# Feed-forward and MLP up projections by seven quarter products instead of eight

## What is computed

```python
h = rms_norm(x, norm_mlp[layer])
x = x + jnp.square(jax.nn.relu(h @ w_up[layer])) @ w_down[layer]      # MLP, 4096 wide
...
def swiglu(h, w_gate, w_up, w_down):
    return (jax.nn.silu(h @ w_gate) * (h @ w_up)) @ w_down
...
c_act = jax.nn.silu(c)
for l in range(DEPTH_2):
    mod = (c_act @ w_ada[l] + b_ada[l]).reshape(B, N_MOD, D_MODEL)    # N_MOD = 9
    h = modulate(rms_norm_2(x, norm_gain[l, 0]), mod[:, 0], mod[:, 1])
    x = x + 0.5 * mod[:, 2][:, None, :] * swiglu(h, ffn_w_gate[l, 0], ffn_w_up[l, 0], ffn_w_down[l, 0])
    ...                                                               # mixer, then the second swiglu
```

## Time and profile before

| | |
|---|---|
| median of 3 runs | 3504.78 us |
| profiled execution, first to last instruction | 3498.8 us |
| PE busy | 3407.7 us (97%), 17034 matmuls |
| POOL busy | 2369.8 us (68%) |
| DVE busy | 1179.6 us (34%) |
| ACT busy | 885.8 us (25%) |
| DMA | 388.09 MB, mean 111 GB/s |

### The profile page before, as it was taken

The page is one execution under the profiler, slowest core; times in us unless marked ns, Lnnn a source line. Parts: engine busy times, 40 slices in busy tenths (PEclk is TensorE's granted clock), DMA queues, the critical chain, the costliest instruction groups (busy, mean ns, idle before and its releaser), DMA issues.

```text
span 3498.8 us, 42521 instructions
## 1 busy us (share of the span) xinstructions
PE 3407.7 (97%) x17034; PEld 2738.7 (78%) x17034; DVE 1179.6 (34%) x2514; ACT 885.8 (25%) x1876; POOL 2369.8 (68%) x1242
## 2 busy tenths in 40 slices
PE   8888999999999999999999999999999999999999
PEld 6655777988898888667779888888887677798887
DVE  6554332433443234442223111332244422241111
ACT  2656551211120102354312000210012543221000
POOL 7515447787778776645677877687775546678775
PEclk9999999999999999999999999999999999999999
DMA  3222213444535442212232222254432122223222
GB/s 142 68 69 82 67 62 108 149 171 170 185 127 204 168 166 94 73 58 85 85 106 96 97 97 96 83 220 165 171 126 73 67 76 79 82 97 106 98 98 73
DMA packets 104773, 388.09 MB, mean 111 GB/s; under 512 B 12017, under 2 KB 12401, under 8 KB 98433
## 3 DMA queue, kind: packets, MB, share of 16 engines
q1 hardware_dynamic: 88272, 292.76, 24.4%
q10 hardware_dynamic: 16304, 92.62, 7.0%
HBM read 383.20 MB, written 2.13 MB: 110 GB/s over the span
## 4 chain that ended last, share of the span: by engine, by line
PE 92%; DVE 4%; ACT 3%; issue 1%; ACTq 0%; DVEq 0%
PE psum L1234 28%; PE psum L1236 27%; PE psum L1235 27%; PE psum L1307 2%; PE psum L1349 2%; PE psum L1324 2%; PE psum L1293 1%; DVE rs_t L1695 1%; ACT s_sb L1477 0%; DVE s_sb L1736 0%; ACT L1477 0%; ACT s_sb L1495 0%; PE psum L1407 0%; PE psum L1285 0%; DVE n_sum L1906 0%
## 5 line engine op out<-in xcount | busy, mean ns | idle before, releaser
L1202 POOL TENSOR_TENSOR w_hi<-raw,ones 128x1024 fp32r<-128x1024 f32 (+2 forms) x593 | 1041.3, 1756 | 990.4 <-PE psum L1236 981.2
L1205 POOL TENSOR_TENSOR w_lo<-raw,w_hi 128x1024 fp32r<-128x1024 f32 (+2 forms) x593 | 1315.1, 2218 | 46.5
L1234 PE MATMUL psum<-h_hi,w_hi 128*128 128x512 f32 (+2 forms) x2912 | 1143.4, 393 | 19.4 <-DVE r L1711 9.4
L1236 PE MATMUL psum<-h_hi,w_lo 128*128 128x512 f32 (+2 forms) x2912 | 1105.3, 380 | 0.0
L1235 PE MATMUL psum<-h_lo,w_hi 128*128 128x512 f32 (+2 forms) x2912 | 1104.8, 379 | 0.0
L1234 PEld LDWEIGHTS psum<-h_hi,w_hi 128*128 128x128 f32 (+1 forms) x2912 | 550.2, 189 | 156.6 <-issue 35.9
L1236 PEld LDWEIGHTS psum<-h_hi,w_lo 128*128 128x128 f32 (+1 forms) x2912 | 549.7, 189 | 106.6
L1235 PEld LDWEIGHTS psum<-h_lo,w_hi 128*128 128x128 f32 (+1 forms) x2912 | 550.9, 189 | 103.3 <-issue 9.0
L1234 PE MATMUL psum<-a_hi,w_hi 128*128 128x512 f32 (+1 forms) x1064 | 392.5, 369 | 0.0
L1235 PE MATMUL psum<-a_lo,w_hi 128*128 128x512 f32 (+1 forms) x1064 | 391.8, 368 | 0.0
L1236 PE MATMUL psum<-a_hi,w_lo 128*128 128x512 f32 (+1 forms) x1064 | 391.8, 368 | 0.0
(11 more groups left out here) (198 smaller groups left out, 3299.5 us busy)
## 6 DMA issues: line engine op xcount, KB each, us to landing
raw<-weights_dram SPq DMA_DIRECT2D x487, 512.0 KB, 3.3
ada_t<-ada_dram ACTq DMA_DIRECT2D x48, 1536.0 KB, 7.1
raw<-weights_dram SPq DMA_DIRECT2D x76, 256.0 KB, 2.6
raw<-weights_dram SPq DMA_DIRECT2D x32, 384.0 KB, 2.9
bias_t<-biases_dram ACTq DMA_DIRECT2D x36, 256.0 KB, 2.9
bias_t<-cum_dram ACTq DMA_DIRECT2D x16, 256.0 KB, 3.9
out_dram<-x SPq DMA_DIRECT2D x8, 256.0 KB, 2.1
raw<-weights_dram SPq DMA_DIRECT2D x4, 408.0 KB, 3.1
```

Of the source, the lines that this page charges most:

```text
L1202: nc.gpsimd.tensor_tensor(high, piece, ones[:, 0:1].to_broadcast([P, n]), ALU.mult)\
L1205: nc.gpsimd.tensor_tensor(w_lo[:, p % NR, 0:n], piece, high.bitcast(F32), ALU.subtract)\
L1234: mm(dst, lh, rh, start=first, stop=False)
L1236: return mm(dst, ll, rh, start=False, stop=last)
```

## The change

Gate and up groups after the first four are made in *sets* of four: two pairs (in a feed-forward part two gates and two ups, in the MLP two and two ups). A pair is a product of a 2 by 2 array of weight quarters (two output chunks by two halves of the 1024 input features) with a 2 by 2 array of quarters of `h` (halves of the features by halves of the tokens), made by seven products instead of eight. A product takes four chunks with three matmuls of 256 columns each (L1538 to L1540), 12 in all, so a set takes 14 products and 168 matmuls of 256 columns where it was 96 of 512. There are 7 sets in the MLP and 10 in each of the four feed-forward parts, 47 in all.

- Sums of quarters of `h` (`t_new`, `t_hi`, `t_lo`) are made once for each norm, in four steps (`tsum`, `tlow`): four DVE instructions of 256 columns, an ACT copy of 1024 and a DVE subtraction of 1024 in each. The scaled input stands in SBUF (`n_out`) instead of PSUM, since it is needed again.
- Sums of weight quarters are made in PSUM banks 0 and 1: ACT moves a quarter there, DVE adds (S3, S1, S2, S4), ACT or POOL makes the high and DVE or POOL the low part of each of the 14 operands. An operand takes one of the six slots (512 columns high, 512 low).
- Partial results are kept by ACT (`keep`) and added by DVE (`c22`, `c1`) ahead of the gate and the product.
- `norm_rest` interleaves four first groups instead of three (banks 6, 7, 4, 5).
- The condition's sums, now two for each load of 1 MB, stand only between down groups (ten in each of three parts of the MLP; 9, 9 and 0, then 9, 9 and 0, then 6, 0 and 0 in the feed-forward parts), and its silu is made in banks 0 and 1 anew for each of these parts. The first two loads are issued behind the last set of the first part.

```diff
@@ norm_rest: the sums of h behind the second half of the norm
+    sums = quarter_sums(m) if m.quartered else iter(())
     for c in range(KC):
         for g in firsts:
             mm(g, c, c + 1, 1)
-        next(second, None)
+        if next(second, None) is None:
+            next(sums, None)
+    for _ in sums:
+        pass
@@
+def with_ada(groups, n, stop):
+    def condition():
+        tick("c_made")
+        put("cond", [take(b) for b in SUM_BANKS], TOTAL["cond_loaded"])
+    out = [condition]
+    for i, g in enumerate(groups):
+        out += [lambda: ada_sum(stop)] * sum(6 * k // n == i for k in range(n)) + [g]
+    return out
@@
+BY = dict(P1=("pool", "pool"), P2=("pool", "pool"), P5=("act", "dve"), P6=("act", "dve"), P7=("act", "pool"),
+          P3=("act", "dve"), P4=("pool", "pool"))
...
+    for what in PRODUCTS:
+        for p in pairs:
+            p.ops[what].done = tick("product_done")
+            put("product", p.ops[what])
...
+            elif what == "P3":
+                p.c1 = tick("combined")
+                put("c1", p)
+                result(p, 0)
+            elif what == "P4":
+                result(p, 1)
@@ ffn
+        for t in range(first, chunks, 2):
+            kinds = [[(kind, l, n, at + t + i) for i in TWO] for kind in ("fg", "fu")]
+            banks = SET_BANKS[(chunks - t) // 2 % 2 == 0]
+            jobs.append(lambda kinds=kinds, t=t, banks=banks: new_set(kinds, ((t, t + 1),) * 2, banks, m))
...
+        if part == 0 and stop:
+            jobs += [ada_load, ada_load]
+        if not closes:
+            groups = down_groups(keys, chunks, "a", (l, 2 * n))
+            jobs += with_ada(groups, ada[part], stop) if ada[part] else groups
@@ where the scaled input stands (norm_tile, which L1671, L1425 and L1678 of before use)
-            return bank(m.nt[c % 2])[:, columns(half)]
+            return n_out[:, c, columns(half)] if m.quartered else bank(m.nt[c % 2])[:, columns(half)]
@@ which steps come when an operand's slot is free (place - 6 used)
+    for step in ORDER:
+        if step[0] in ("prep", "mm", "product"):
+            yield from ready()
+        yield step
@@ PE
+            def product(op):
+                pair, what, m = op.pair, op.what, op.pair.norm
+                E.wait_at(op.low)
...
+                for k in range(KC // 2):
+                    if what in ("P1", "P2", "P3"):
+                        c, cs = k + KC // 2 * (what != "P1"), columns(int(what == "P3"))
+                        hi, lo = h_hi[:, c, cs], h_lo[:, c, cs]
+                    else:
+                        E.wait_ge("t_lo", m.sums + k + 1)
+                        j = dict(P5=0, P6=1, P7=2, P4=3)[what]
+                        hi, lo = t_hi[:, k, j, :], t_lo[:, k, j, :]
...
+                    mm(dst, wh[:, w], hi, start=start, stop=False, skip_group_check=True)
+                    mm(dst, wh[:, w], lo, start=False, stop=False, skip_group_check=True)
+                    ins = mm(dst, wl[:, w], hi, start=False, stop=stop, skip_group_check=True)
@@ ACT
+            def operand(op):
+                gate, up = SETS[op.pair.made // 8]
+                if (op.what, op.pair) == ("P2", up):
+                    move(gate)
+                elif (op.what, op.pair) == ("P5", gate):
+                    move(up)
@@ DVE
+            def quarter_sum(m, k):
...
+                if k >= 2:
+                    E.wait_ge("t_lo", m.sums + k - 1)
+                v.tensor_tensor(t[0], n_out[:, k, far], n_out[:, k, near], ALU.subtract)
...
+            def first_sums(pair):
+                a, _, c, d = quarters(pair)
+                E.wait_at(loaded(pair.pieces[0]))
+                E.wait_ge("moved", pair.moved)
+                v.tensor_tensor(c, sums(pair), a, ALU.add).then_inc(sem["sums_made"], 1)
+                E.wait_at(summed(pair, "S3"))
+                v.tensor_tensor(sums(pair), sums(pair), d, ALU.add).then_inc(sem["sums_made"], 1)
+            def operand(op):
+                gate, up = SETS[op.pair.made // 8]
+                if (op.what, op.pair) == ("P2", up):
+                    first_sums(gate)
+                elif (op.what, op.pair) == ("P5", gate):
+                    first_sums(up)
+                if op.low[0] == "low_dve":
+                    E.wait_at(op.high)
+                    v.tensor_tensor(low_of(op), sums(op.pair), high_of(op).bitcast(F32), ALU.subtract)
+                if op.what in ("P5", "P6"):
+                    next_sum(op.pair, "S2" if op.what == "P5" else "S4")
```

More of the change, by code:

```diff
@@ L308, with quartered @@
     used: int = 0
+    products: int = 0
+    sums: int = 0
+    @property
+    def quartered(self):
+        return self.which == ("mlp",) or len(self.which) == 2 and self.which[1] != 1
     def square_bank(self, c, half):
@@ L376, in norm_chunks, with quarter_sums @@
         yield c
+def quarter_sums(m):
+    m.sums = TOTAL.get("t_lo", 0)
+    for k in range(KC // 2):
+        assert tick("t_sum") == tick("t_hi") == m.sums + k + 1
+        put("tsum", m, k)
+        yield k
+        if k:
+            put("tlow", m, k - 1, tick("t_lo"))
+    put("tlow", m, KC // 2 - 1, tick("t_lo"))
 def in_banks(groups, banks):
@@ new lines @@
+@dataclass(eq=False)
+class Operand:
+    what: str
+    pair: object
+    place: int
+    high: tuple = None
+    low: tuple = None
+    done: int = 0
+@dataclass(eq=False)
+class Pair:
+    side: int
+    banks: tuple
+    norm: Norm
+    made: int
+    pieces: tuple = ()
+    before: tuple = ()
+    ops: dict = None
+    former: object = None
+    sums_before: tuple = None
+    moved: int = 0
+    p1: int = 0
+    p5: int = 0
+    u2: int = 0
+    c22: int = 0
+    c1: int = 0
+@dataclass(eq=False)
```

420 lines of the change are left out of this document (326 added, 94 removed).

## The result

The changed kernel takes 3593.22 us (median of 4 runs, 3590.35 to 3604.75), the kernel before on the same chip 3502.61 us (4 runs). The ratio is 1.0263, with a 95% interval of 1.0245 to 1.0281: 2.6% slower. The forecast was 3557 us, range 3482 to 3610: sign and range held, and 36 of the 91 us were missing. The time lies nearer to the 3608 us of the rival in which every later set waits than to the forecast; only the trace tells the two apart.

The account below looks back on a forecast made before the run. PE, busy 97% of the span, was taken to bound the kernel. 3498.8 - 75.2 + 1.6 + 16 + 65.6 + 10 + 34 = 3550.8 us for the span, 6.0 more for the median: 3557 us, range 3482 to 3610.

Parts of the forecast that it names:

- the rival in which every later set waits: Feed-forward sets: if each hand-over costs 0.15 us more, sets lose 2.1 us, 51 us more, 3608 us; chance 0.14.
- The matmuls: PE in the 47 sets: 1.60 us gained each, 75.2 us; halves in the fourth first group cost 1.6 us.
- Inside the sets: Operand waits within sets: POOL 8 us over 12 parts, MLP's second P5 6, late `a_lo` 2; sum 16 us.
- The norms: Two PE waits at each of five norms, for bank 5 and for quarter sums (`t_lo`) in P5: 65.6 us.
- The condition's sums: Down groups: additions that empty banks stand behind load sums, so PE waits 34 us; 8 with quick loads.
- the loads are quick: Rival on the condition's loads: at 3.3 us each they cost 8 us, 3531 us; lower part of the forecast's 0.60.
- The clock: Idle PE then runs at half clock, one stretch a norm and a few in down groups: 10 us, bounds 0 and 30.
- The signs that I named: PE idle 4 to 5 us before first groups are well begun, released by addition or `n_sum`; 7 to 12 in P5, by `t_lo`.
- sign of a wrong forecast: PE idle under 3 us a norm at `t_lo`, or waits for POOL's or DVE's operands above 30 us in all.
- DVE in time at the norms: Rival at the norms: DVE makes quarter sums early enough, norm and clock terms go, 3481 us, faster; chance 0.20.

Follow-up runs that it names:

- x11: Kernel before the change, feed-forward sets changed except plain first sets; early loads, first-half `h_lo` from PSUM, coefficient instructions spread: 3466.3 us, 0.9906 of before.
- x5: Changed kernel with the first set after each of five norms made of four plain groups of 512 columns: 3566.8 us, 1.0191 of the kernel before.
- x4: Changed kernel with the eight small coefficient instructions issued one by one, a down group apart: 3583.8 us, 1.0239 of the kernel before.
- x9: Changed kernel with product P2 of both pairs made three times in the first set after each norm: 3589.7 us, 1.0261 of the kernel before.
- x8: Changed kernel with the MLP as before; in feed-forwards a plain first set after the norm and two early loads: 3489.7 us, 0.9965 of before.

## Why the prediction was right, and what it sized wrong

- *The matmuls*, 75.2 us: 0.120 us a step in the sets, as forecast. x11, where the waits are few, is 34 us faster than before.
- *Inside the sets*, 16 us: 7.1 for POOL as worked out (12 x 0.6, which I had rounded up to 8), and the MLP's second P5 9.9 us (two waits of 1.7 and 1.6 in three parts; I had one of 2.1). With the late `a_lo` some 21. The rival with waits in every later set is refuted: feed-forward sets wait for nothing but POOL.
- *The norms*, 65.6 us: 14 in first halves where I had 23, 28.5 at `t_lo` and P5 where I had 43: 42 us of recorded waits. Both mechanisms are there. The lock meets only some of the `h_lo`: I had each of the first five wait, and in the MLP's norm two of eight take 2.3 and 2.2 us, two 0.9 and four 0.48. At `t_lo` the price was nearly right: 5.25 us of rows in ff(0,0), but 6.3 us of delay where I had 7.4. That the order of place 1 makes these waits, with an idle DVE in it, is read from the timelines; x5 takes the wait away by giving PE other work, and no run moved the quarter sums ahead of the products.
- *The condition's sums*, 34 us: 43 us of waits in the down groups. By MLP parts it was 8.2, 8.1 and 14.8 us where I had 11.2, 6.5 and 6.5; the feed-forwards had 12 where I had 10. Three things were off. The first two loads of a phase I gave 9.3 us, but 2 MB at the 289 GB/s that I worked out are 7.3 us, and 7.3 (ff(0,0)) and 7.9 (MLP) is what they took. A single load takes 6.1 us, not the 5.2 I took between two rows, so *the loads are quick* is refuted; the page DMA: Bandwidth & Descriptors of the Trainium skill (Bandwidth, Measured) has 6.15 us for 1 MB, a busy time of transfers that GpSimd issued, where the 6.1 here run from issue to landing beside the weights; the two are near each other. And I costed only the two instructions of a sum: the eight `coefs` behind the 24th load, with a port lock each, I did not step through, though the earlier trace rows price such instructions. By x4 they are 9 us of the whole, less than the 14 us wait suggests.
- *The clock*, 10 us: **the step that was sized wrong.** I took "one such stretch a norm and a few in the down groups", some of it hidden. There were 17 stretches at half clock that cost 1.4 to 2.9 us each, 33.7 us in all and above the 30 that I had as a bound: 11 us in five behind the waits in P5, 7 in four in the norms' first halves, 15 in eight in the down groups. That the one behind the P5 wait is "mostly hidden, since PE waits anyway" was wrong: after the last wait PE is never waiting again, and P5 to P7 run at half rate (21 matmuls in 5 us above). x9 shows it goes with the idle time.
- *Around the waits*: 25 us. The waits in my sum are delays of PE, and a row records less than the delay, some 0.25 us less each; so about 18 of the 25 belong to the wait terms, which then measured 125 us for my 116, and only the short gaps were in no term.
- *The balance.* The waits in my sum, 115.6 us, were 107 in the trace: the condition's too low, the norms' too high. Clock + 24, around the waits + 25, outside + 2, waits - 8.5 make the 42.6 us between 3550.8 and the profiled span of 3593.4. Against the median 36 are left: I added 6.0 us because the median before stood that far above one profiled span, but each run's time is only some 1.8 us above its own span (3595.18 against 3593.4), and the median after lies 0.2 us below that span.
- *The signs that I named*: PE's first wait in a norm was 1.6 to 3.3 us, not 4 to 5, and the waits in P5 5.3 us in a feed-forward and 8.3 in the MLP, not 7 to 12; both were released as I said. Neither sign of a wrong forecast came: more than 3 us at `t_lo` in each norm, and 20.1 us for POOL's and DVE's operands, under 30.
- *DVE in time at the norms* did not happen. The waits in the norms, 8.5 us each, are above the 4.7 from which I had the change slower, so the sign does not hang on the term that I sized wrong. Take most of the norms' and the condition's waits away, with 11 of the 47 sets, and the change is faster (x8 to x11).

## What to carry to other kernels

When the engine that bounds a kernel stops even for two or three microseconds, price three things: the wait, the restart behind it, and the work that follows at half clock; here the second and third added half again to the first (25 and 34 us to 107). Before work moves to an in-order engine, list everything on it behind the last thing that is awaited, the smallest instructions too, and give each that has no input in PSUM the length of the POOL instruction that it can meet. A saving spread over many short pieces (1.6 us in 20) is worth taking only in the places where every operand is early: here 36 sets of 47, with plain work right behind each norm.
